# Trainium2: the eight sample memories of an mLSTM head in the first eight slots of its loop, a whole one per slot, instead of spread over fourteen

## What is computed

```python
num = a[..., None] * jnp.einsum('bhtd,bhdv->bhtv', qc, C) + jnp.einsum('bhts,bhsv->bhtv', s, vc)
...
C_new = decay[..., None, None] * C + jnp.einsum('bhsd,bhsv->bhdv', wk, vc)
```

## Time and profile before

| | |
|---|---|
| median of 3 runs | 3069.36 us (3067.78 to 3074.34) |
| profiled execution | 3065.72 us, of which the span of the trace is 3063.9 us |
| PE busy | 2959.9 us, 97% of the span |
| DVE, ACT, POOL busy | 55%, 28%, 35% |
| the four heads | 133.67, 133.71 and 133.73 us for heads 0 to 2; head 3 runs on into the output projection |

### The profile page before, as it was taken

One profiled execution on the slowest core, in us unless ns is written; L12 is line 12 of the kernel. 1 busy time (PEld: TensorE's weight loads), 2 busy tenths in 40 slices (PEclk: granted clock), 3 DMA queues, 4 the chain that ended last, 5 costly groups with the idle time before them and its releaser, 6 DMA issues.

```text
span 3063.9 us, 50087 instructions
## 1 busy us (share of the span) xinstructions
PE 2959.9 (97%) x19348; PEld 2752.6 (90%) x19348; DVE 1687.7 (55%) x2551; ACT 844.0 (28%) x1491; POOL 1068.1 (35%) x742
## 2 busy tenths in 40 slices
PE   7998899999999999999989999998999999999997
PEld 7886689999999998999977778777998999999997
DVE  4877545544444446443357887878326344444445
ACT  4000533222222225111143544434006122222211
POOL 3232032554555614333300101112332356555453
PEclk9999999999999999999989999999999999999999
DMA  8556211111111112433244664749311111111121
GB/s 229 138 148 143 80 52 42 35 48 48 55 48 55 53 30 63 169 112 105 106 161 159 219 220 159 279 148 325 120 43 34 50 56 48 37 39 54 48 76 57
DMA packets 276673, 313.20 MB, mean 102 GB/s; under 512 B 25733, under 2 KB 217477, under 8 KB 275314
## 3 DMA queue, kind: packets, MB, share of 16 engines
q1 hardware_dynamic: 257777, 250.82, 26.7%
q10 hardware_dynamic: 13048, 40.28, 3.4%
q0 software_dynamic: 5712, 20.19, 1.8%
HBM read 219.91 MB, written 92.19 MB: 102 GB/s over the span
## 4 chain that ended last, share of the span: by engine, by line
PE 83%; DVE 8%; ACT 4%; issue 3%; PEld 1%; DMA 1%; POOL 0%; SPq 0%; ACTq 0%; another core or an unknown queue 0%; DVEq 0%; PEldq 0%; POOLq 0%
PE ps L449 20%; PE ps L450 19%; PE ps L451 19%; PE ps L884 4%; PE ps L883 3%; PE ps L885 3%; PE ps L2581 2%; PE ps L1577 2%; PE ps L1512 2%; PE ps L1533 1%; DVE CT L2059 1%; PE ps L1603 1%; PE ps L1535 1%; PE ps L1534 1%; DVE CB L3011 1%
## 5 line engine op out<-in xcount | busy, mean ns | idle before, releaser
L449 PE MATMUL ps<-AH,WH 128*128 128x352 f32 x3072 | 999.3, 325 | 5.2 <-POOL WL L436 2.0
L451 PE MATMUL ps<-AH,WL 128*128 128x352 f32 x3072 | 985.6, 321 | 0.0
L450 PE MATMUL ps<-AL,WH 128*128 128x352 f32 x3072 | 985.6, 321 | 0.0
L449 PEld LDWEIGHTS ps<-AH,WH 128*128 128x128 f32 x3072 | 576.9, 188 | 30.5 <-issue 22.6
L450 PEld LDWEIGHTS ps<-AL,WH 128*128 128x128 f32 x3072 | 577.9, 188 | 1.1 <-issue 0.2
L451 PEld LDWEIGHTS ps<-AH,WL 128*128 128x128 f32 x3072 | 577.3, 188 | 0.0
L434 POOL TENSOR_SCALAR WH<-RAW 128x1024 fp32r<-128x1024 f32 x152 | 182.5, 1200 | 970.2 <-PEq L456 741.1
L436 POOL TENSOR_TENSOR WL<-RAW,WH 128x1024 fp32r<-128x1024 f32 x152 | 399.3, 2627 | 12.7
L1107 DVE TENSOR_TENSOR X<-X,ps 128x352 f32<-128x352 f32 x432 | 225.2, 521 | 264.4 <-PE ps L885 134.0
L998 ACT ACTIVATE SGF<-ps 128x352 f32<-128x352 f32 x192 | 88.8, 462 | 679.6 <-PE ps L451 679.5
L1059 DVE TENSOR_TENSOR HR<-SGF 128x352 f32<-128x352 f32 x144 | 92.7, 644 | 288.4 <-ACT SGF L998 286.5
(11 more groups left out here) (397 smaller groups left out, 4925.8 us busy)
## 6 DMA issues: line engine op xcount, KB each, us to landing
RAW<-in_ffn_w SPq DMA_DIRECT2D x128, 512.0 KB, 3.8
CT<-in_state_mlstm_C SPq DMA_DIRECT2D x32, 1024.0 KB, 6.7
out_C_s<-CT SPq DMA_DIRECT2D x32, 1024.0 KB, 6.6
RAW<-in_ml_w_in SPq DMA_DIRECT2D x32, 512.0 KB, 3.9
RAW<-in_conv_w_pw SPq DMA_DIRECT2D x24, 512.0 KB, 8.2
STK<-u_scratch SPq DMA_DIRECT2D x64, 184.0 KB, 3.9
xc_scratch<-XC ACTq DMA_DIRECT2D x16, 528.0 KB, 2.7
so_scratch<-SO ACTq DMA_DIRECT2D x16, 528.0 KB, 3.7
```

The lines of the kernel that those rows point to most:

```text
L449: pe.matmul(ps[:, bank, 0:CW], wh[:, k, cols], hi[:, k, cs], start=(k == 0), stop=False)
L450: pe.matmul(ps[:, bank, 0:CW], wh[:, k, cols], lo[:, k, cs], start=False, stop=False)
L451: mm = pe.matmul(ps[:, bank, 0:CW], wl[:, k, cols], hi[:, k, cs], start=False, stop=(k == nk - 1))
```

## The change

The table `HALVES` gives slot q, for q = 0 to 7, both halves of sample q, and the slots 8 to 15 nothing. Before, slots 0 and 1 took one half each, slots 2 and 3 two each, and slots 4 to 13 one each. In POOL's list `vm(7)` moves ahead of two DMA issues, since sample 7 is now wanted earlier.

```diff
-        HALVES = {0: (0,), 1: (1,), 2: (2, 3), 3: (4, 5)} | {q: (q + 2,) for q in range(4, 14)}
+        HALVES = {q: (2 * q, 2 * q + 1) for q in range(8)}
...
-            for b in range(3, 7):
+            for b in range(3, 8):
                 vm(b)
             out_store(pool, h, 0)
             xo_load(pool, h, 2)
-            vm(7)
             out_store(pool, h, 1)
```

## The result

The changed kernel takes 3160.51 us (median of 4 runs, 3158.75 to 3167.48) against 3068.57 for the kernel before beside it: 92 us more, ratio 1.0301 with a 95% interval of 1.0288 to 1.0314. Slower was forecast, but by 59 us, and 3160.5 lies above the range of 3098 to 3152.

A forecast was written before the change was run, and what follows sets the result against it. PE, busy for 97%, and the DMA-fed ring of three C buffers were taken as both near their limit. Waits, clock and tail summed to +14.7 us a head, 59 over four: 3128 us, range 3098 to 3152.

The forecast's parts named there:

- The ring: Three C buffers filled and emptied by DMA pace slots 5 to 7: +40 to +80 us, chance 0.70.
- Rival B: The buffers turn faster, as a DMA stream without gaps: 5.4 us a head, +22 us, chance 0.12.
- Rival C: The tail suffers too: DVE and ACT pace slots 8 to 13, gaps cost clock; +80 us and beyond, chance 0.11.
- Rival D: Faster: PE's waits in slots 8 to 15 and for the load vanish; -17 us, chance 0.03.
- Rival E: No difference: the 3 us of slots 0 and 1 return in the tail, gaps hide; chance 0.04.
- Slots 0 to 3: Slots 0 and 1 take 3.0 us more for four halves; slots 2 and 3 keep their 13.3 us.
- Load 4: Sample 4's load, issued at 1795, lands 6.0 us later; slot 4 starts at 1801.3.
- Load 5: Sample 5's load, behind CPO and XCH, lands 18.2 us after 1795; PE waits 6.3 us at slot 5.
- The turns: Slots 6 and 7: each store takes 8.9 us, each load 6.3; PE waits 1.5 and 3.2 us.
- The clock: Gaps ahead of slots 5 and 7 each lose 1.7 us; the first is absorbed, the last adds 1.7.
- Slots 8 to 15: The tail falls from 42.13 to 34.5 us without three samples, PE's idle 3.2 us left as it is.
- The test in the profile: PE waits about 6, 1.5 and 3 us in slots 5 to 7; no new wait in slots 8 to 15.

The follow-up runs named there:

- run 1: The changed kernel with samples 3 to 7 loading, and every store writing, only two of C's four blocks: 3114.09 us, ratio 1.0145.
- run 3: The changed kernel with the XCH load (WR in the last head) issued behind the load of sample 7: 3137.35 us, ratio 1.0214.
- run 5: The changed kernel with both half of C's blocks moved (loads of samples 3 to 7, all stores) and XCH behind load 7: 3084.63 us, ratio 1.0047.
- run 7: The kernel before with whole samples in slots 0, 2, 3, 4, 6, 8, 10 and 12, where each began before: 3070.94 us, ratio 1.0008.
- run 11: The changed kernel with both CPO and XCH issued behind the load of sample 7: 3138.80 us, ratio 1.0219.
- run 4: The changed kernel with unused matrix products ahead of the waits for loads 4 to 7, keeping PE busy: 3156.78 us, ratio 1.0282.
- run 9: The changed kernel with VectorE's skip and gate of token blocks 0 and 1 one slot later in heads 0 to 2: 3156.66 us, ratio 1.0281.
- run 6: The changed kernel with whole samples only in slots 0 to 3, then one half a slot in slots 4 to 11: 3105.76 us, ratio 1.0119.
- run 12: The changed kernel with the store of sample b issued ahead of the load of sample b + 2: 3161.06 us, ratio 1.0302.
- run 14: The kernel before with the store of sample b issued ahead of the load of sample b + 2: 3091.89 us, ratio 1.0076.
- run 2: The kernel before with samples 3 to 7 loading, and every store writing, only two of C's four blocks: 3069.24 us, ratio 0.9997.

## Why the prediction was wrong in size and right in kind

**What bounds the kernel, and the sign: right.** The ring set the pace of slots 4 to 7. Runs 1, 3 and 5 show it by halving the bytes or moving XCH away, and run 7 by asking for the samples at the old times. Rival B, a faster ring, fell: the last load landed 4 us later than forecast, not 7.6 sooner, since each load waits until a store has landed, which is what the prediction put against B. Rival C came nearest, as the last paragraphs say. Rival D, faster, was far off: even without any wait for a load (run 5) the new lists are 15 us slower. Rival E fell with it.

**Slots 0 to 3: right.** Slot 2 starts 10.86 us after slot 0 (7.92 before), +2.9 for the forecast +3.0. Slots 2 and 3 took 1822.58 - 1809.18 = 13.4 us for 13.3 (1822.58 is the start of slot 4 less its wait, 1825.97 - 3.39). The price of a dense slot was 5.7 us; in run 5, where nothing waits, slots 4 and 5 take 5.7 and 5.6.

**Load 4: mis-sized.** The step "lands 6.0 us later" failed: it took 7.8 us in head 1, and in the kernel of run 3 8.6. The 6.0 of rows 6 was a load whose store followed 1.7 us later, not at once. It was also issued 0.8 us later after slot 0 than forecast. PE waited 3.4 us, not 1.0. Over heads 0 to 3 the load took 6.4, 7.8, 7.5 and 6.9 us. A store issued with it makes part of that, as the other pairs show (6.2 to 6.9). Why head 1's takes up to 2 us more stays open: run 11 excludes CPO and XCH. It cost little in the end, since slot 5 began when load 5 had landed, 39.7 to 40.5 us after slot 0 in all four heads. Where load 4 was early, PE waited longer in slot 5 (8.6 us in head 0).

**Load 5: mis-sized.** It landed 20.7 us after load 4's issue (1838.8 - 1818.08); the forecast was 18.2, from the 19.6 of rows 4 and 5 less a gap. There was hardly a gap to save: over those 19.6 us before, the DMA share was 0.96 at 353 GB/s, and over the 20.7 now it is 0.97 at 344. With load 4 issued 0.8 us late, load 5 was 3.3 us late.

**The turns: right in size, but not for the reason given.** Forecast 8.9 us a turn and 6.3 for the load. Measured: 9.2 between the last two loads, and 6.6 and 6.8. The prediction held that two transfers overlap and so beat two in a row. "DMA: Bandwidth & Descriptors" of the Trainium skill, section "Bandwidth", has 6.15 us for 1 MB alone, by which two in a row would make an estimated 12.3. The trace does not agree, and it decides: alone, the store took 4.2 us and the load 5.0, and in a row that is the same 9.2.

**The clock: right that the next wait absorbs most of it, too small in extent.** Forecast were two gaps at 1.7 us, one of them absorbed. The granted clock was 0.80 over slots 4 to 7, with slow products behind all four gaps. PE was busy there for 30.4 us, and for 22.65 in the same slots of run 5, so the low clock cost 7.8 us of PE's time:

```profile
1806.63:1829.60 22.97, 22.65 (x137) 16.00 (x137) 21.36 (x37) 10.21 (x21) 2.06 (x3) 1.00 0.81 271
```

Run 4 gave most of the clock back and won 1.3 to 3.3 us a head in three heads. The last gap is absorbed by nothing, as forecast: slot 7 took 1864.28 - 1857.39 = 6.9 us from its wait on, and 5.3 in run 5. That the clock falls behind each wait is what the Trainium skill says under "TensorE: Matmul & The Clock Gate", section "HAM oscillation — how this bites in real kernels", of a loop that waits for a transfer at each turn; here the trace agrees, with 0.80 against 1.00 in run 5, where no load is waited for.

**The sum of these:** slot 8 starts 1864.28 - 1798.32 = 65.96 us after slot 0, where it was 40.10 before: +25.9. The forecast was 1838.5 - 1816.15 = +22.4. So loads and clock cost 3.5 us a head more than forecast, 14 of the missing 33: the last load landed 4.0 us late, and slot 7 gave back 0.5.

**Slots 8 to 15: the step that failed most.** The step was "without three samples 34.5", that is, 7.6 us given back, with PE's idle time left as it was. From slot 8 to the next slot 0 the head gave back only 25.9 - (156.95 - 133.73) = 2.6 us. This is the other 5 us a head, 20 us in all. Run 5 splits it without the clock: PE's busy time in the tail is 38.97 - 33.08 = 5.9 us less, not 7.6, and its idle time 6.6 us instead of 3.2. In the prediction this stood as a bound of 3 us and as a part of rival C, with 0.11; it should have been in the sum. PE waits there 3.6 us for VectorE's sums (SQH). Its longest wait in the loop of before was for such sums too, and rows 3 and the prediction left it out:

```profile
PE ps L1458 <- DVE SQD L2209: 1.6, 1, 1.6
```

My reading is that the statistics take ScalarE and VectorE as long as before when the slots become shorter. It is argued and not shown as a whole: run 9 moved one step and got back 1.3 us a head, while other waits grew. The changed kernel itself has besides a clock of 0.96 in its tail, but that costs little: from slot 8 to the next slot 0 it takes 91.0 us, and run 5 at a clock of 1.00 takes 90.4.

**The test in the profile.** PE's waits for the loads of samples 5, 6 and 7 were forecast at 11.0 us a head (6.3, 1.5 and 3.2) and came out at 7.6 (4.2, 2.0, 1.4). With load 4 it is 12.0 forecast and 11.0 measured in head 1, and 49 us over the four heads for 40 to 50. That these sums nearly agree, although the parts do not, was chance: the low clock fills with slow products what would otherwise be waiting. The sign "no new wait in slots 8 to 15" failed, by the 3.6 us for the sums, and that was the sign named for rival C.

## What to carry to other kernels

When work with its own transfers is packed closer, count the bytes per stretch first: before, these buffers were filled and emptied in slots whose DMA share was already 1.00, and a transfer asked for earlier does not come earlier. Then count the turns of the ring: where a load waits for the landing of a store, 2 MB took 9.2 us here while the DMA engines were busy for only 0.77 of it. Size a pair of transfers by a pair in the trace, never by one that ran alone. And do not credit the stretch that work leaves with its full price: its remaining chains have lengths of their own, and what was hidden under the work becomes a wait.

## What the runs showed of the hardware that was not expected

A load of 1 MB issued 0.4 us ahead of a store of 1 MB landed after 6.2 to 6.9 us in most places. For sample 4 it took 7.8 and 7.5 in heads 1 and 2 of the changed kernel, and 8.4 to 9.0 in head 1 of runs 3, 6, 9 and 11, which stays unexplained. Alone, such a load took 5.0 us and such a store 4.2. The order within a pair decides who pays: behind the store the load mostly took 7.3 to 7.6 us, and the store ahead of it about 5.0 (runs 12 and 14). This is part of why the swap costs the kernel before 24 us over the four heads, while half the bytes gain it nothing (run 2).
